# Two transformer blocks on one core: experts numbered anew on the chip, one program per weight buffer, outputs summed in PSUM

## What is computed

```python
grp = argmax(xf @ w_coarse + b_coarse)              # 1 of 4 groups
fine = (xf @ w_fine + b_fine)[.., grp]              # 8 experts per group
top_p, top_i = lax.top_k(softmax(fine), 2)          # 2 of them per token
weights = p_grp * top_p / sum(top_p)
for each expert e:                                  # 32 experts, 1024 -> 512 -> 1024
    hid = silu(xb @ w_gate[e]) * (xb @ w_up[e])
    out = hid @ w_down[e]
y = sum over a token's two experts of weight * out
x = x + gt2 * y;  return rms_norm(x, g_final)
```

## Time and profile before

| what | before |
|---|---|
| median of three runs (lowest, highest) | 1120.13 us (1119.55, 1121.98) |
| time of the profiled execution | 1122.88 us |
| its span, first to last instruction | 1121.2 us |
| PE, DVE, ACT, POOL busy | 75%, 35%, 35%, 3% |
| granted clock of PE, mean | 0.908 |
| first gate and up matmul of the experts | 635.62 us |
| last one starts | 1084.60 us |

### The profile page before, as it was taken

The page is one execution under the profiler, slowest core; times in us unless marked ns, Lnnn a source line. Parts: engine busy times, 40 slices in busy tenths (PEclk is TensorE's granted clock), DMA queues, the critical chain, the costliest instruction groups (busy, mean ns, idle before and its releaser), DMA issues.

```text
span 1121.2 us, 20073 instructions
## 1 busy us (share of the span) xinstructions
PE 839.7 (75%) x7685; PEld 670.2 (60%) x7686; DVE 394.2 (35%) x562; ACT 393.2 (35%) x535; POOL 28.5 (3%) x84
## 2 busy tenths in 40 slices
PE   6998897999999987997776754575565655665626
PEld 5997686899999977995374532343333323333313
DVE  3654877655555466445845300000000000000002
ACT  5433673556455335444723311112111111112103
POOL 3000000000000000000000000000000000000000
PEclk9999999899999999899888888899878889988769
DMA  6676042256546452576628355699999999999750
GB/s 237 231 257 223 1 151 76 78 186 224 183 154 221 153 163 98 178 220 255 227 79 342 127 204 227 269 426 426 427 426 428 426 427 424 395 416 374 325 224 38
DMA packets 88259, 278.78 MB, mean 249 GB/s; under 512 B 7279, under 2 KB 67098, under 8 KB 70810
## 3 DMA queue, kind: packets, MB, share of 16 engines
q1 hardware_dynamic: 87518, 276.84, 64.0%
q10 hardware_dynamic: 700, 1.36, 0.3%
HBM read 277.13 MB, written 1.05 MB: 248 GB/s over the span
## 4 chain that ended last, share of the span: by engine, by line
PE 17%; DMA 16%; issue 7%; DVE 5%; ACT 3%; PEld 2%; PEldq 2%; SPq 0%; POOLq 0%; DVEq 0%; POOL 0%
DMA Whi<-in_w_up 12%; PE bank L1576 8%; DMA Wlo<-in_w_up 4%; PE bank L1593 2%; PEld bank L1576 1%; PE bank L1659 1%; PEldq L1561 1%; PE bank L1584 1%; PE bank L360 1%; PE bank L362 1%; PE bank L361 1%; DVE V L2276 1%; ACT V L1123 1%; DVE rms L2137 1%; PE bank L1602 1%
## 5 line engine op out<-in xcount | busy, mean ns | idle before, releaser
L360 PE MATMUL bank<-R_r,Whi_r 128*128 128x256 f32 x864 | 251.4, 291 | 27.6 <-DVE R_r L1903 7.3
L361 PE MATMUL bank<-R_r,Whi_r 128*128 128x256 f32 x864 | 249.2, 288 | 0.0
L362 PE MATMUL bank<-R_r,Whi_r 128*128 128x256 f32 x752 | 216.1, 287 | 0.0
L360 PEld LDWEIGHTS bank<-R_r,Whi_r 128*128 128x128 f32 x864 | 170.6, 197 | 31.0 <-issue 25.2
L361 PEld LDWEIGHTS bank<-R_r,Whi_r 128*128 128x128 f32 x864 | 170.8, 198 | 0.1
L362 PEld LDWEIGHTS bank<-R_r,Whi_r 128*128 128x128 f32 x752 | 147.9, 197 | 0.0
L1576 PE MATMUL bank<-Whi,S 128*32 128x256 f32 x1152 | 85.8, 464 | 67.8 <-DMA Whi<-in_w_up 36.8
L1576 PE MATMUL bank<-Wlo,S 128*32 128x256 f32 x1024 | 79.9, 480 | 68.8 <-DMA Wlo<-in_w_up 47.2
L2276 DVE TENSOR_TENSOR V<-V,bank 64x256 f32<-64x256 f32 x34 | 14.4, 424 | 302.3 <-ACT V L1123 302.3
L1576 PEld LDWEIGHTS bank<-Whi,S 128*32 128x32 f32 x1152 | 49.1, 132 | 100.2 <-issue 84.6
L1576 PEld LDWEIGHTS bank<-Wlo,S 128*32 128x32 f32 x1024 | 44.6, 137 | 100.2 <-issue 88.9
(11 more groups left out here) (396 smaller groups left out, 1238.8 us busy)
## 6 DMA issues: line engine op xcount, KB each, us to landing
Whi<-in_w_gate SPq DMA_DIRECT2D x14, 2048.0 KB, 12.4
Whi<-in_w_up SPq DMA_DIRECT2D x14, 2048.0 KB, 16.9
Whi<-in_w_down SPq DMA_DIRECT2D x14, 2048.0 KB, 18.6
Wlo<-in_w_gate SPq DMA_DIRECT2D x14, 2048.0 KB, 16.0
Wlo<-in_w_up SPq DMA_DIRECT2D x14, 2048.0 KB, 20.5
Wlo<-in_w_down SPq DMA_DIRECT2D x14, 2048.0 KB, 23.6
Wlo<-in_w_in SPq DMA_DIRECT2D x24, 1024.0 KB, 5.3
Wlo<-in_w_gate_up SPq DMA_DIRECT2D x22, 1024.0 KB, 6.3
```

Source lines behind the costliest of these rows:

```text
L360: pe.matmul(o, w_hi[:, c], tile(x_hi, k), start=(k == 0), stop=False)
L361: pe.matmul(o, w_hi[:, c], tile(x_lo, k), start=False, stop=False)
L362: mm = pe.matmul(o, w_lo[:, c], tile(x_hi, k), start=False, stop=(k == KT - 1))
```

## The change

Four parts.

1. **Numbering.** A table is made on the chip by small matmuls and DVE steps: used experts get consecutive ranks, experts 0 and 1 keep ranks 0 and 1 (they are loaded ahead) and unused ones come last. `tbl` has five rows by rank: expert, first slot, count, windows, and windows of all ranks before. The buffer is chosen by rank. `now`, the number of the window over all experts, is what all semaphores count, so unused ranks need no drains and no waits.
2. **One copy of the program per buffer.** The loop over `w` runs from 0 to 7 for each used rank, on PE, ACT, DVE and POOL, with one test in it; there is no copy for single windows any more.
3. **Combination.** Banks 4 to 7 hold the sum for all tokens during the whole stage. Per window DVE compares the window's slot numbers with `slotrow` and gets a 0/1 matrix `oh` and the weight of each slot; it scales the down output by weight and by `gt2` (laid out by rows, `gt2band`); ACT and DVE split it in a high and a low part; `combine` adds it in with 16 matmuls of 32 rows, and runs in the next window, between its gate and up matmuls and its transposes. Banks: transposes in 2, down in 3. Removed: `Pw` and its transposes, the two transposes after down, `ysT`, `ystok` and the 32 records and matmuls of the end; the adds at the end are eight of 128x256.
4. **Ahead of the experts**: ACT makes eight diagonal blocks of `gt2` and then eight of slots and weights, before its copies of `xsT`; PE spreads them over rows with 8 + 8 matmuls, and zeroes the four banks with four matmuls.

The diff, cut to what matters:

```diff
-                    if i is not None and name == "wg":
-                        sp.wait_ge(*upto(f"gu_free{par}", i))
-                    if i is not None and name == "wd":
-                        sp.wait_ge(*upto(f"d_free{par}", i))
+                    if used is not None and name == "wg":
+                        sp.wait_ge(*upto("gu_done", used))
+                    if used is not None and name == "wd":
+                        sp.wait_ge(*upto("yw_done", used))
                     sp.dma_start(Wx[par][:, at:at + KT * DE].rearrange("p (a n) -> p a n", **dims),
                                  rows).then_inc(sem(f"{name}_full{par}"), 16)
...
-                    count = sp.value_load(tbl[0:1, bass.ds(i * 2 + (NE + par), 1)],
-                                          min_val=0, max_val=T)
-                    with sp.If(count > 0):
-                        expert_load(i * 2 + par, par, i)
...
+                    windows = sp.value_load(tbl[0:1, bass.ds(i * 2 + (NW_AT + par), 1)],
+                                            min_val=0, max_val=NWIN)
+                    with sp.If(windows > 0):
+                        expert = sp.value_load(tbl[0:1, bass.ds(i * 2 + (EID + par), 1)],
+                                               min_val=0, max_val=NE - 1)
+                        used = sp.value_load(tbl[0:1, bass.ds(i * 2 + (WB_AT + par - 1), 1)],
+                                             min_val=0, max_val=MAXWIN)
+                        expert_load(expert, par, used)
...
+            act.wait_ge(*upto("xtok_done", 4))
+            for k in range(KT):
+                act.activation(gt2_diag[:, k * P:(k + 1) * P], ident[:, :], ACT.Copy,
+                               scale=modT[:, 5 * KT + k:5 * KT + k + 1]).then_inc(sem("gt2_diag"), 1)
+            act.wait_ge(*upto("slots_set"))
+            for n, at in enumerate((12, 13, 7, 8)):
+                for t in range(TT):
+                    act.activation(slot_diag[:, (n * TT + t) * P:(n * TT + t + 1) * P], ident[:, :],
+                                   ACT.Copy, scale=rs[:, at * TT + t:at * TT + t + 1]
+                                   ).then_inc(sem("slot_diag"), 1)
...
             for k in range(KT):
+                if k == 2:
+                    pe.wait_ge(*upto("counts_set", 3))
+                    pe.matmul(bank[7][0:NE, 0:3], tri_lt[0:NE, 0:NE], counts3, start=True, stop=True
+                              ).then_inc(sem("before_done"), 1)
+                if k == 3:
+                    pe.wait_ge(*upto("slot_diag", 4 * TT))
+                    for n in range(4 * TT):
+                        mm = pe.matmul(bank[4 + n // 4][:, (n % 4) * P:(n % 4 + 1) * P], ones[:, 0:P],
+                                       slot_diag[:, n * P:(n + 1) * P], start=True, stop=True)
+                    mm.then_inc(sem("slot_rows"), 1)
+                if k == 5:
+                    pe.wait_ge(*upto("perm_set"))
+                    pe.matmul(bank[7][:, 16:16 + NV5 * NE], ones[0:NE, 0:P], permv, start=True, stop=True
+                              ).then_inc(sem("table_done"), 1)
...
+            pe.wait_ge(*upto("zero_set"))
+            pe.wait_ge(*upto("slot_rows_out", 3))
+            pe.wait_ge(*upto("tbl_ready"))
+            pe.wait_ge(*upto("slot_ix"))
+            for b in range(4):
+                mm = pe.matmul(bank[4 + b][:, :], zero_r, Psel_r[:, 0, :], start=True, stop=False)
+            mm.then_inc(sem("acc_zero"), 1)
...
+            def combine(last=False):
                 for t in range(TT):
+                    for part in (yp_hi, yp_lo):
+                        for g in range(P // WIN):
+                            band = slice(g * WIN, (g + 1) * WIN)
+                            mm = pe.matmul(bank[4 + g][:, t * 256:(t + 1) * 256],
+                                           oh[band, t * P:(t + 1) * P], part[band, :], start=False,
+                                           stop=last and t == TT - 1 and part is yp_lo)
+                return mm
...
             with pe.Fori(0, NE // 2) as i:
                 for par in range(2):
-                    count = pe.value_load(tbl[0:1, bass.ds(i * 2 + (NE + par), 1)],
-                                          min_val=0, max_val=T)
-
-                    pe.wait_ge(*upto(f"yt_out{par}", i))
-                    pe.wait_ge(*upto(f"byt_out{par}", i * (NWIN - 1)))
-                    with pe.If(count > WIN):
-                        window(par, "", i + 1, count)
...
-                            for name in ("gu_done", "ht_done", "y_done", "yt", "gu_free",
-                                         "d_free"):
-                                pe.drain().then_inc(sem(f"{name}{par}"), 1)
-                        for name in ("gu_done", "ht_done", "y_done", "yt"):
-                            pe.drain().then_inc(sem(f"b{name}{par}"), NWIN - 1)
-            for par in range(2):
-                pe.wait_ge(*upto(f"yt_out{par}", NE // 2))
...
+                        before = pe.value_load(tbl[0:1, bass.ds(i * 2 + (WB_AT + par), 1)],
+                                               min_val=0, max_val=MAXWIN)
+                        with pe.Fori(0, NWIN) as w:
+                            with pe.If(windows > w):
+                                now = before + w + 1
+                                pe.wait_ge(*upto(f"wg_full{par}", i * 16 + 16))
+                                pe.wait_ge(*upto(f"wu_full{par}", i * 16 + 16))
+                                pe.wait_ge(*upto("xw", now))
+                                for k in range(KT):
+                                    for g in range(4):
+                                        c = (WG, WU)[g // 2] + k * DE + (g % 2) * 256
+                                        mm = pe.matmul(bank[par][g * WIN:(g + 1) * WIN, 0:256],
+                                                       xw[par][:, k * WIN:(k + 1) * WIN], W[:, c:c + 256],
+                                                       start=(k == 0), stop=(k == KT - 1))
+                                mm.then_inc(sem("gu_done"), 1)
+
+                                pe.wait_ge(*upto("yp_lo", before + w))
+                                combine().then_inc(sem("comb"), 1)
+
+                                pe.wait_ge(*upto("hid", now))
+                                for c in range(2):
+                                    at = par * T + c * P
+                                    mm = pe.transpose(bank[2][:, at:at + P], hidw[:, c:2 * P:2],
+                                                      ident[:, :])
+                                mm.then_inc(sem("ht_done"), 1)
+                                pe.wait_ge(*upto("ht_out", now))
+                                pe.wait_ge(*upto(f"wd_full{par}", i * 16 + 16))
+                                for f in range(DE // P):
+                                    at = (f % 2) * 2 * WIN + (f // 2) * WIN
+                                    for g in range(4):
+                                        mm = pe.matmul(
+                                            bank[3][g * WIN:(g + 1) * WIN, par * T:(par + 1) * T],
+                                            hidT[:, at:at + WIN],
+                                            W[:, WD + f * D + g * 256:WD + f * D + (g + 1) * 256],
+                                            start=(f == 0), stop=(f == DE // P - 1))
+                                mm.then_inc(sem("yw_done"), 1)
+            pe.wait_ge(*upto("y_all"))
+            combine(True).then_inc(sem("comb_done"), 1)
...
+                            with dve.If(windows > w):
+                                now = before + w + 1
+                                dve.wait_ge(*upto("sil", now))
+                                dve.tensor_tensor(hid, sil, bank[par][2 * WIN:P, 0:256], ALU.mult
+                                                  ).then_inc(sem("hid"), 1)
+
+                                dve.tensor_copy(ix_now, slot_ix[:, bass.ds(i * 2 * NWIN + w + par * NWIN, 1)]
+                                                ).then_inc(sem("ix_now"), 1)
+                                dve.wait_ge(*upto("comb", now))
+                                dve.wait_ge(*upto("ix_now", now))
+                                dve.tensor_scalar(oh, slotrow[:, 0:T], ix_now, None, ALU.is_equal
+                                                  ).then_inc(sem("oh_first"), 1)
+                                dve.scalar_tensor_tensor(out=scratch, in0=slotrow[:, 0:2 * T],
+                                                         scalar=ix_now, in1=slotrow[:, 2 * T:4 * T],
+                                                         op0=ALU.is_equal, op1=ALU.mult,
+                                                         accum_out=wt_now).then_inc(sem("wt_now"), 1)
+                                dve.wait_ge(*upto("oh_first", now))
+                                dve.scalar_tensor_tensor(out=oh, in0=slotrow[:, T:2 * T], scalar=ix_now,
```

(76 more changed lines are left out.)

339 lines of the change are left out of this document (115 added, 224 removed).

## The result

The changed kernel takes 1151.95 us (median of four runs, 1147.01 to 1154.17), the kernel before 1120.09 us (four runs). The ratio is 1.0275, 95% interval 1.024 to 1.0311: 31.9 us slower. The forecast was slower by 12.9. The profiled execution has a span of 1150.4 us.

The account below looks back on a forecast made before the run. PE's sequencer was taken to bound at 15.7 us a rank, against a 14.8 us load. 640.6 + 50 + 392.5 + 20 + 31 = 1134.1, 12.9 above the old span, added to median 1120.13: forecast 1133.0 us, range 1106 to 1158.

Parts of the forecast that it names:

- ranks 0 and 1: First two ranks of the experts' stage: 27.4 us and 20.7, plus 1.8 for fetching code; together 50 us.
- 22 ranks of one window: Ranks of one window after the first two: 15.7 us each, from 5.3, 1.83, 0.47 and 8.1.
- Which engine bounds: Experts' loop: PE's sequencer becomes the bound, by 0.9 us a rank over the 14.8 us load; empty pass 0.78.
- 5.3 (gate and up at about the mean of the earlier trace): Term in a one-window rank: gate and up take 5.3 us of the 15.7.
- neither rival: The two rivals: control cheaper than 8.1 us, chance 0.28; the combination not hidden, chance 0.12.
- The start: Work ahead of the experts: first gate and up 5.0 us later, at 640.6; ends +2 and +8.
- The combination hidden: In each window: 16 matmuls take 0.92 us and hide in the 0.95 PE waits for the product; 0 added.
- That rival, 0.12: Combination not hidden: 1.0 to 1.5 us in each of 34 windows, 1167 to 1183 us at most; chance 0.12.
- Control cheaper, the load bound, 1076 us: Experts' loop: control below 8.1 us; with steps below 13.5 the load bounds throughout, time 1076 us; chance 0.28.
- Consecutive numbers: Near the experts' end: consecutive ranks take away the late load, some 15 to 20 us of waiting.
- The end: From the last gate and up to the span's end: about 31 us, before 36.6.
- A code fetch of 1.8 us at the first ranks: At the first two ranks: 1.8 us added for fetching code once, far less than the 7.61 before.

Follow-up runs that it names:

- experiment 1: Changed kernel with window loops ending at the rank's own number of windows on PE, ACT, DVE and POOL, inner test gone: 1075.08 us, 0.957 of the kernel before.
- experiment 2: Changed kernel with window loops ending at the rank's windows on PE alone; ACT, DVE and POOL keep eight turns: 1078.93 us.
- experiment 4: Changed kernel with only the window loops' end changed on all engines: 1128.01 us with seven turns, 1077.76 us with four.
- Experiment 6: Changed kernel with one added float32 matmul of 256 columns in each of PE's eight turns: 1120.51 us, 0.998 of the kernel before.
- experiment 7: Kernel before, profiled again: 1119.22 us; experiment 1's kernel again: 1075.01; the same with gt2's diagonal blocks, matmuls and copy made later: 1071.54.
- experiment 3: Changed kernel with 15 of the combination's 16 matmuls left out in every window: 1150.13 us, 1.0246 of the kernel before.
- experiment 8: Experiment 1's kernel with the experts' old numbers, all 32 counted as used for the ranks: 1088.01 us, 0.970 of the kernel before.
- experiment 5: Changed kernel with 12 added float32 matmuls of 256 columns after each window's down: 1251.39 us.

## Why the prediction was right in kind and wrong in size

The sum of the prediction against the changed kernel's profiled execution:

| term | predicted us | measured us |
|---|---|---|
| first gate and up | 640.6 | 645.7 |
| ranks 0 and 1 | 50.0 | 51.8 (to 697.6) |
| 22 ranks of one window | 345.4 (15.7 each) | 357.4 (16.24 each) |
| 3 ranks of two windows | 67.1 | 65.7 |
| last gate and up to the end | 31.0 | 29.7 |
| span | 1134.1 | 1150.4 |

The spans are 16.3 us apart, the time and its forecast 19.0. The other 2.7 come from the reference: the profile of before was 2.75 us above its median, that of the change lies at its own (1152.23 and 1151.95), and I had added a difference of spans to a median.

- **Which engine bounds: right.** It is PE's sequencer, not its array and not the load, and it is the empty passes (experiments 1, 2 and 4). The price of a pass was taken as 0.78 from an old loop and is 0.74. From down's start to the next gate and up I had 8.57 us; it is 8.2 or 8.6 (808.64 to 816.84, 823.76 to 832.40).
- **The step that failed is "5.3 (gate and up at about the mean of the earlier trace rows)".** It is 5.97. The earlier trace rows themselves say 5.41; the rest is the clock. I carried a duration from windows with 2 to 5 us of idle array ahead of them over into a loop with 5.6 to 6.7 us of it ahead of every rank from the third on, which my own sum had just made. 0.67 us in 22 ranks are 15 us, of which control gives back 3. What the idle array does to the clock was priced at nothing, and neither rival held it. Experiment 6 shows that it is the clock: with the idle stretch filled, gate and up fell to 4.2 us.
- **The start:** 5.0 us for the work ahead of the experts was right, 4.7 measured (experiment 7). The other 5.4 us of this profile arose ahead of the mark, where the change adds nothing but two small matmuls (0.3 us), and where the granted clock was lower in this execution. How much of it the other three executions had is not known.
- **The combination hidden: right** (experiment 3); 0.74 us, where I had 0.92 by one row and about half of 1.48, which is 0.74, by the other. That rival, 0.12, falls.
- **Control cheaper, the load bound, 1076 us:** not what happened. When the passes were taken away the kernel stood at 1075, so that rival's sum for a kernel bound by the load was sound; a pass simply wasn't cheaper than I had read it. The Trainium skill's figures for branches ("Advanced Engine Details and Errata", Control Flow Timing), 51 ns for a jump and 108 for a compare and branch, aren't what this loop shows: its taken compare and branch takes 0.21 us, one that isn't taken 0.07 to 0.09.
- **Consecutive numbers:** I had 15 to 20 us of late load; 13 were measured (experiment 8).
- **The end:** 31 forecast, 29.7 measured. The terms that I had written down add up to 30.1.
- **A code fetch of 1.8 us at the first ranks: not there.** The two took 51.8 us instead of 50, but none of the 448 branches of the window loop and its test lasted longer than 0.23 us:

```profile
L1587 PEldq COMPARE_BRANCH  x224: 86/218/227, 653.5 to 1133.4; - x112
L1588 PEldq COMPARE_BRANCH  x224: 71/214/216, 644.6 to 1133.0; - x112
```

The clock took that time too. The first gate and up of ranks 0 and 1 were 5.31 and 6.47 us, where I had put 3.66 for both:

```profile
645.74 5.31 PE L1596 MATMUL bank<-Whi,S 128*32 128x256 f32 x64 [3.10 <-POOL S L787]
674.09 6.47 PE L1596 MATMUL bank<-Wlo,S 128*32 128x256 f32 x64 [4.85 <-issue]
```

That is 4.5 us more, and smaller terms that came out shorter bring the sum to 3.7 over 48.1, the two ranks without the fetch. So the same step failed here. The 7.61 us of the earlier trace rows remain unexplained; I had written that nothing was loading then, but the DMA moved 2.5 MB during that branch.
- **Two readings that change nothing in the sum:** the slices at about 426 GB/s in the earlier trace rows are eight, not ten, and the two behind them have 395 and 416.

My second forecast on the clock, in experiment 5, failed too: I had 3 us at most for a full queue in one rank and 1200 us at most for the time; 34 windows of up to 3 us would have been 102 already.

## What to carry to other kernels

Count what the sequencer of the busiest engine does in a turn that does no work, and multiply by the turns: one empty pass of 0.74 us, seven to a rank, outweighed all that the change saved here. A loop whose bound is known in a register needs no empty passes, and here the loop's bound and the test in it, changed on four engines, made 1152 us into 1075. Where a sum makes an engine idle in one piece, the durations behind that piece have to be looked up at the clock that such a piece leaves, not at the old mean.

## What the runs showed of the hardware that was not expected

- Extra work can pay: 224 float32 matmuls of 256 columns in the idle stretches took the granted clock from 0.76 to 0.96 (780 to 955 us) and 31 us off the time.
- The sequencer of PE can run only so far ahead of the array. With down's 32 records it went on 0.5 us after their start; with 24 more records behind them, whose weights have 128 columns instead of 32, it was held for 2.8 us longer.
- Sixteen matmuls of 32 rows and 256 columns in four row groups and four banks take 0.74 us together, one alone takes 0.38.
- Ahead of the experts nearly the same instructions put the routing's mark anywhere from 613.8 to 619.6 us after the span's start; one kernel, profiled twice, had it at 617.1 and 615.1.
